# A transformer pair on one core: another order of the first products, the bias table's load, and the conditioning work beside attention

## The reference

```python
# first_block
mod = (c_act @ ada_w[i] + ada_b[i])[:, None, :]          # conditioning: 6 vectors of 1024
sh1, sc1, g1, sh2, sc2, g2 = jnp.split(mod, 6, axis=-1)
h = rmsnorm(x, mix_norm_pre[i]) * (1.0 + sc1) + sh1
y = windowed_gqa_sink(h, w_qkv, w_o, sink, rel_bias)     # 16 heads, bias table from rel_bias
x = x + g1 * rmsnorm(y, mix_norm_post[i])
h = rmsnorm(x, ffn_norm_pre[i]) * (1.0 + sc2) + sh2
y = (jax.nn.silu(a) * b) @ w_out                         # a, b = split(h @ w_in)
x = x + g2 * rmsnorm(y, ffn_norm_post[i])
# second_block: 2 layers; each ends in peer(): 16384 experts, 8 heads x top 16 for each token,
# whose rows are gathered from memory
```

## Time and profile before

| | us |
|---|---|
| median of 3 runs | 2074.97 (2071.8 to 2075.92) |
| the profiled execution, its own time | 2070.76 |
| span from its first to its last instruction | 2069.0 |
| PE / DVE / ACT / POOL busy | 1744.1 / 1469.1 / 919.5 / 613.1 |
| first Q, K, V matmul; first unit of attention on DVE; `post` | 37.5; 70.7; 156.9 |
| FFN's first product; its second; end of the second's matmuls | 171.5; 301.6; 363.3 |

### The profile page before, as it was taken

How to read it: one execution, slowest core, us unless ns; L and a number is a source line. 1 busy time by engine, 2 the same in 40 slices (tenths; PEclk the granted TensorE clock), 3 DMA queues, 4 the chain that set the end, 5 groups by cost and what they waited for, 6 DMA issues and landing times.

```text
span 2069.0 us, 21998 instructions
## 1 busy us (share of the span) xinstructions
PE 1744.1 (84%) x6989; PEld 1026.8 (50%) x6989; DVE 1469.1 (71%) x3271; ACT 919.5 (44%) x2397; POOL 613.1 (30%) x575
## 2 busy tenths in 40 slices
PE   3888999899888798987887787998999978778876
PEld 2657998788767354533322323464555423223322
DVE  6778877888876587766677767527776767667675
ACT  3555444444472344453444444334444444444443
POOL 1250000000002354433434343114455433433431
PEclk9998999999999999999999999999999999999999
DMA  9654768566645999999999999859999999999996
GB/s 380 267 193 182 265 245 305 215 256 243 242 166 205 418 421 422 421 421 417 421 421 422 421 421 421 325 188 384 408 418 421 421 422 421 422 421 421 422 421 256
DMA packets 114651, 723.24 MB, mean 350 GB/s; under 512 B 11484, under 2 KB 13300, under 8 KB 34024
## 3 DMA queue, kind: packets, MB, share of 16 engines
q0 software_dynamic: 75152, 541.35, 63.1%
q1 hardware_dynamic: 39384, 180.50, 23.5%
HBM read 720.72 MB, written 1.08 MB: 349 GB/s over the span
## 4 chain that ended last, share of the span: by engine, by line
DMA 38%; PE 30%; DVE 18%; ACT 7%; issue 4%; POOL 3%; SPq 0%; ACTq 0%; DVEq 0%
DMA X<-in_k_uv,EI 24%; DMA Z<-in_k_uv,EI 12%; PE PS L2266 12%; PE PS L1956 4%; PE PS L1958 4%; PE PS L1957 4%; DVE junk L1943 3%; DVE W L1568 3%; PE PS L2242 3%; DVE WL L1580 2%; POOL X L1074 2%; ACT WH L1083 1%; PE PS L2283 1%; ACT L1083 1%; ACT E L1083 1%
## 5 line engine op out<-in xcount | busy, mean ns | idle before, releaser
L2266 PE MATMUL PS<-X,dg 128*128 128x512 f32 x1380 | 666.7, 616 | 129.2 <-ACT dg L1083 128.5
L1943 DVE CUSTOM_DVE_ANT_0 junk<-H,X 128x1024 f32<-128x1024 f32 x345 | 421.9, 1223 | 240.6 <-DMA X<-in_k_uv,EI 235.9
L1074 POOL DMA_INDIRECT X<-in_k_uv,EI x345 | 364.8, 1057 | 512.5 <-PE PS L2266 378.1
L2266 PEld LDWEIGHTS PS<-X,dg 128*128 128x128 f32 x1380 | 249.2, 193 | 504.7 <-ACT dg L1083 289.1
L1083 ACT ACTIVATE CF<-DOT 128x1 f32<-128x1 f32 x512 | 103.6, 202 | 661.2 <-DVE DOT L1943 660.3
L2266 PE MATMUL PS<-Z,dg 128*128 128x512 f32 x480 | 237.6, 622 | 56.4 <-ACT dg L1083 55.9
L1943 DVE CUSTOM_DVE_ANT_0 junk<-H,Z 128x1024 f32<-128x1024 f32 x120 | 146.8, 1223 | 95.6 <-DMA Z<-in_k_uv,EI 93.8
L1083 ACT ACTIVATE dg<-CP,CG 128x128 f32<-128x128 f32 x512 | 205.5, 401 | 18.2 <-PE PS L2266 1.5
L1956 PE MATMUL PS<-XH,WH 128*128 128x256 f32 x592 | 174.5, 295 | 16.2 <-DVE XL L1483 14.8
L2266 PEld LDWEIGHTS PS<-Z,dg 128*128 128x128 f32 x480 | 84.5, 192 | 189.9 <-ACT dg L1083 123.2
L1957 PE MATMUL PS<-XL,WH 128*128 128x256 f32 x592 | 170.5, 288 | 0.0
(11 more groups left out here) (319 smaller groups left out, 2509.6 us busy)
## 6 DMA issues: line engine op xcount, KB each, us to landing
W<-in_k_ada SPq DMA_DIRECT2D x58, 1024.0 KB, 5.4
W<-in_k_win SPq DMA_DIRECT2D x15, 1024.0 KB, 5.7
Y<-in_k_ada SPq DMA_DIRECT2D x14, 1024.0 KB, 6.3
W<-in_k_ffi SPq DMA_DIRECT2D x14, 1024.0 KB, 5.5
Y<-in_k_ffi SPq DMA_DIRECT2D x8, 1024.0 KB, 6.6
W<-in_peer_wq SPq DMA_DIRECT2D x8, 1024.0 KB, 14.0
W<-in_ffn_w_out SPq DMA_DIRECT2D x6, 1024.0 KB, 7.6
W<-in_ab_w_out SPq DMA_DIRECT2D x6, 1024.0 KB, 6.2
```

The lines of the kernel that those rows point to most:

```text
L1074: e.indirect_dma_start(out=WS[k][:, :], out_offset=None, in_=I[f"k_uv{ly}"][:, :], in_offset=bass.IndirectOffsetOnAxis(ap=EI[t][:, j:j + 1 ...
L1943: e.tensor_tensor_reduce(junk, H[:, t, :], d[:, 0:D], 1.0, 0.0, ALU.mult, ALU.add, DOT[:, j:j + 1]).then_inc(v_dot, 1)
L2266: p = e.matmul(PS[:, 2 * t + q, :], dgb[n % 4][:, :], d[:, D + q * 512:D + (q + 1) * 512], start=(j == 0), stop=(j == 127))
```

## The change

1. **Start of the program.** `be` stands behind `ldw 1`, and POOL now waits there until `ldw 1` has landed. `ada 6 1`, `ada 7`, `mod 1` and `g 1` stand ahead of both halves of `split 0`, so on DVE they come before the first low part of weights. `split 0 0` stands behind `xt` of chunk 3, `split 0 1` behind chunk 5.
2. **Block 0** runs its quarters in the order 0, 2, 1, 3: both halves of the result over chunks 0 to 3, then both over 4 to 7. The second half is summed in another PSUM bank (2), from which the copy on ACT reads it.
3. **Attention.** The halves of blocks 6 and 7 move from steps 3 to 6 to steps 7, 8, 10 and 11, those of block 8 from 13, 14 to 14, 15. The `ada` operations move so that most steps hold either one half or one `ada`; the last steps hold two or three. `mod 3` and `g 2` stand just before the last output block.
4. **`ada 21`** moves from right before `post` into the FFN's first product, at blocks 3 and 7 of it, and **`ada 22`** from the FFN's second product to blocks 11 and 15.
5. **The FFN's second product.** Block i waits for activation pair i, no longer for all 11.

```diff
-    P("be")
     P("xp", 0, 7, 3)
...
     P("ldw", 1)
+    P("be")
     for c in range(3):
         P("xt", 0, c, first[c])
-    P("split", 0, 0)
+    ada(6, 1)
     for c in range(3):
         P("xl", 0, c)
-    ada(6, 1)
+    P("ada", 7, 0)
+    P("ada", 7, 1)
+    P("mod", 1)
+    P("g", 1)
     P("xt", 0, 3, first[3])
+    P("split", 0, 0)
     P("xl", 0, 3)
...
+        for q in (0, 2, 1, 3) if n == 0 else range(4):
+            P("gq", n, q, n)
...
-    halves = {1: (5, 0), 2: (5, 1), 3: (6, 0), 4: (6, 1), 5: (7, 0), 6: (7, 1), 13: (8, 0), 14: (8, 1), 17: (9, 0),
+    halves = {1: (5, 0), 2: (5, 1), 7: (6, 0), 8: (6, 1), 10: (7, 0), 11: (7, 1), 14: (8, 0), 15: (8, 1), 17: (9, 0),
...
-    adas = {0: [22, 23], 1: [24], 2: [25]} | {n: [n + 20] for n in range(6, 22)}
...
+            18: [34], 19: [35, 36, 37], 20: [38, 39], 21: [40, 41]}
...
-    ada(21, 0)
-    ada(21, 1)
     P("post", 0, 0)
...
-    late = [22, 23] + list(range(32, 39))
+    late = [23] + list(range(32, 39))
...
                     w.wait_ge(d_td, 16)
+                    w.wait_ge(*slot("ldw", 1)[1:])
                     e.dma_start(BE[:, :, :], bass.AP(tab_d, 0, [[1, 128], [512, 16], [1, 384]])).then_inc(d_be, 16)
...
-                        w.wait_ge(a_ff, 11)
-                        w.wait_ge(v_ffl, 11)
+                        w.wait_ge(a_ff, n - FO + 1)
+                        w.wait_ge(v_ffl, n - FO + 1)
```

More of the change, by code:

```diff
@@ L111, in make_plan @@
     P("ldw", 1)
+    P("be")
     for c in range(3):
         P("xt", 0, c, first[c])
-    P("split", 0, 0)
+    ada(6, 1)
     for c in range(3):
         P("xl", 0, c)
-    ada(6, 1)
+    P("ada", 7, 0)
+    P("ada", 7, 1)
+    P("mod", 1)
+    P("g", 1)
     P("xt", 0, 3, first[3])
+    P("split", 0, 0)
     P("xl", 0, 3)
-    P("split", 0, 1)
-    P("ada", 7, 0)
     for c in (4, 5):
@@ L124, in make_plan @@
         P("xl", 0, c)
-    P("ada", 7, 1)
-    P("mod", 1)
-    P("g", 1)
+    P("split", 0, 1)
     for c in (6, 7):
@@ L134, in make_plan @@
         ada(8 + n, 0)
-        gemm(n, n)
+        for q in (0, 2, 1, 3) if n == 0 else range(4):
+            P("gq", n, q, n)
         P("evac", n)
@@ L144, in make_plan @@
     fill |= {9 + 4 * i + q: [(WO + i, q)] for i in range(3) for q in range(4)}
-    halves = {1: (5, 0), 2: (5, 1), 3: (6, 0), 4: (6, 1), 5: (7, 0), 6: (7, 1), 13: (8, 0), 14: (8, 1), 17: (9, 0),
+    halves = {1: (5, 0), 2: (5, 1), 7: (6, 0), 8: (6, 1), 10: (7, 0), 11: (7, 1), 14: (8, 0), 15: (8, 1), 17: (9, 0),
               18: (9, 1), 20: (10, 0), 21: (10, 1)}
-    adas = {0: [22, 23], 1: [24], 2: [25]} | {n: [n + 20] for n in range(6, 22)}
+    adas = {0: [22, 23], 3: [24], 4: [25], 5: [26], 6: [27], 9: [28], 12: [29], 13: [30], 16: [31, 32], 17: [33],
+            18: [34], 19: [35, 36, 37], 20: [38, 39], 21: [40, 41]}
     for n in range(22):
@@ L169, in make_plan @@
             P("gc", 0)
-        elif n == 20:
-            P("mod", 3)
-            P("g", 2)
         if n < 16:
@@ L177, in make_plan @@
     P("ldw", FI + 1)
+    P("mod", 3)
+    P("g", 2)
     gemm(WO + 3)
-    ada(21, 0)
-    ada(21, 1)
     P("post", 0, 0)
@@ L187, in make_plan @@
     P("silu")
-    at = {i: d for d, i in enumerate((i for i in range(22) if i % 4 != 3), 48)}
+    at = {i: d for d, i in enumerate((i for i in range(21) if i % 4 != 3), 48)} | {
+        3: 42, 7: 43, 11: 44, 15: 45}
     for i in range(22):
@@ L191, in make_plan @@
         P("ldw", n + 2)
-        if i in at and at[i] < 64:
+        if i in at:
             ada(at[i] // 2, at[i] % 2)
@@ L203, in make_plan @@
         P("ldw", n + 2)
-        if i < 9:
+        if i < 8:
             ada(late[i], 0)
@@ L1182, in _ @@
                             o = QT[:, 2 * QKV_ORDER[n] + m, :].rearrange("p (t n) -> p t n", t=2)[:, :, ::-1]
-                            q = act(o, PS[:, b, m * 256:(m + 1) * 256].rearrange("p (t n) -> p t n", t=2), ACT.Copy,
+                            z = PS[:, b + (2 * m if n == 0 else 0), m * 256:(m + 1) * 256]
+                            q = act(o, z.rearrange("p (t n) -> p t n", t=2), ACT.Copy,
                                     scale=0.125)
@@ L1978, in to_t @@
                     z = slice(k * 256 + m * 128, k * 256 + m * 128 + 128)
-                    p = mm3(PS[:, b, m * 256:(m + 1) * 256], h[:, z], l[:, z], xh[:, k, :], xl[:, k, :], k == 0, k == 7)
+                    p = mm3(PS[:, b + (2 * m if n == 0 else 0), m * 256:(m + 1) * 256], h[:, z], l[:, z], xh[:, k, :],
+                            xl[:, k, :], k == 0, k == 7)
                 return p
@@ L2070, in _ @@
                             take(b)
+                            if n == 0:
+                                take(2)
+                                free[2] = [(a_ev, nth.ev[0])]
                         p = to_t(n, 0, b, q) if QKV_ORDER[n] < 5 else to_n(n, 0, b, q)
```

## The result

The changed kernel takes 2082.89 us (median of 6 runs, 2081.78 to 2086.7), the kernel before 2075.44 (6 runs, 2071.8 to 2076.54): ratio 1.0042, 95% interval 1.0029 to 1.0055, so 6 to 11 us slower. The prediction was 2071.5, range 2066.5 to 2076. Both the sign and the range missed.

What follows compares the result with a forecast made beforehand. Landing of gathered expert rows (36% of the span) is untouched; the front is bound stage by stage by differing engines and loads. Terms -2.8 + 1.1 + 0.45 - 2.27, taken as 3.5 off median 2074.97, give 2071.5 us; range 2066.5 to 2076.

Steps and rivals of the forecast that it cites:

- Block 0: Start of the program: PE begins about 37.6, runs unbroken and ends at 45.6 instead of 51.88, 6.2 us earlier.
- The loads: Before attention: `ada 11`'s load lands at 65.6, so DVE's first unit starts 2.8 us earlier; bounds 1.5 to 6.2.
- What an earlier start is worth later: From first unit to kernel end: whatever the front gains or loses was taken to arrive at the end unchanged.
- Attention: Steps 3 to 15 with the moved halves: together 1.1 us later (0.0 to 2.6), including 0.75 for PE's lower clock.
- The end of attention: Step 16 to `post`: 0.45 us later; bounds 1.5 earlier to 1.5 later.
- The FFN's second product: Starts at once without PE's wait for the last activations: 2.27 us earlier; bounds 1.5 to 2.3.
- The FFN's first product: Bound by PE, with over 1 us of DVE slack per 5.77 us, so four more products cost nothing.
- the late table: Slower rival, before attention: bias table lands near 85, first unit 14 us later than today, 2088 us; chance 0.08.
- the rival in which attention costs more: PE stays at the lower level in steps 9 to 11, or sums' order breaks: net gain 0 to 1.5; chance 0.20.

Runs made afterwards that it cites:

- e8_cb: Kernel before with the new start alone, and POOL's two broadcasts issued only after `ada 11`'s load has landed: 2073.67 us, ratio 0.9994.
- e10_all: Kernel before with the new start, broadcasts behind `ada 11`'s load, wait per activation pair, and `ada 21`, `ada 22` whole in blocks 7, 15: 2069.6 us, ratio 0.9969.
- e7_warm: `e3_att` with 12 more matmuls, whose sum nobody reads, at the end of each of attention steps 6, 7 and 8: 2082.05 us, ratio 1.0025.
- e3_att: Kernel before with the new attention tables and the new place of `mod 3` and `g 2` alone: 2080.4 us, ratio 1.0024.
- e6_715: Changed kernel with both halves of `ada 21` in block 7 and both of `ada 22` in block 15: 2074.24 us, ratio 0.9994.
- e5_hold: Kernel before with the halves of `ada 24` and `ada 25` reordered, so one slot is held four blocks, no work added: 2081.82 us, ratio 1.003.

## Why the prediction was wrong, point by point

**Block 0: right.** No gap, PE from 37.51 (I had 37.6), copy at 45.74 (45.6).

**The loads: right mechanism, half the size.** `ada 11` binds, and the table lands at 62.9 (61 to 63). Predicted 65.6 for the load, measured 66.4 to 67.2 in four traces. My sum had 24.32 + 1.05 = 25.37 MB moved at that time; in the changed kernel it was 26.12 MB at 67.2 us. Nearly all of POOL's was in by then (4.39 of 4.45 MB), as the sum had it; the 0.8 MB too many are the hardware queue's (21.68 MB, where I had 20.89), from loads issued behind `ada 11`'s, which I had left out. `e8_cb` and `e10_all` show that the broadcasts are worth 1 to 1.7 us, where I had 2.6 (65.6 against 63.0). First unit 69.10 on average of these four, 70.58 in the six without the new start: 1.5 earlier, not 2.8. That is my lower bound.

**What an earlier start is worth later: not in the sum at all.** I carried the gain of the first unit to the end unchanged. With the old tables, the stretch from first unit to `as` 15 took 63.1 us on average of four traces with the old start (62.2 to 64.5) and 64.7 of four with the new (64.5 to 65.1). The new start was 2.6 us ahead at the first unit, 2.2 at `as` 14 and 1.0 at `as` 15.

**Attention: the right term, priced at its low end.** Steps 3 to 6 were 2.85, 3.81, 2.68 and 2.85 us (I had 2.9, 3.7, 2.75, 2.75), the six with a half 5.15 to 5.36 (5.14), step 12 3.55 (3.55), step 13 3.21 (3.2). Step 9 took 5.64, for which I had 3.55, and "up to 2.6" if PE came into it cold, of which I took 0.75. `e7_warm` shows it was that; it took 3.56 there. New tables against old, with the old start: `as` 0 to 15 in 65.3 us (`e3_att`) against 63.1; I had 1.1.

**The end of attention: right.** From `as` 15 to `post` 25.3 us on average of three traces of the changed kernel's plan, 24.9 of five of the old: +0.4, predicted +0.45. The trace that I had read has 24.0, the low end of these five (24.0 to 25.6); that is also why 156.85 was early.

**The FFN's second product: right.** Its wait is gone, and nothing took its place.

**The FFN's first product: the step that failed.** It reads: "DVE has over 1 us of slack in each of its 5.77 us, so four more products cost nothing". DVE's time was the wrong account. The halves that moved there keep a slot from the load to the second half, for four blocks, and the loads behind them in the queue wait. The term was 0 and measured 11.3 (139.13 against 127.86). Whether the moved loads find their slots free, and whether the loads behind them do, I had asked for attention ("all slots free many microseconds ahead") and not here. All the range's bounds came from other terms, and the slower rival, the late table, was a mechanism that did not happen.

By averages of traces: -1.5 (first unit), +2.5 (`as` 0 to 15, 65.6 against 63.1), +0.4 (to `post`), +8.4 (FFN to its second product, 139.1 against 130.7 on average of five), together +9.8; the interval of the medians is 6 to 11. Without what the slots cost, the prediction would have come out within its range, on the side of its high end (`e6_715`: 2074.24), but not by its forecast: a gain of some 1 us, as in the rival in which attention costs more, since the start gave 1.5 instead of 2.8 and attention cost 2.5 instead of 1.1.

## What to carry to other kernels

Where loads take a ring of slots in turn, count for each load how many steps lie between the last use of its slot and its own first use, before and after a move. One operation in two halves far apart, or one load more that shifts the ring, can starve a stage in which every engine but the one that bounds it has slack.

A gain ahead of a stage is worth what the waits behind it leave. Follow it step by step: here 2.2 of 2.6 us were still there at `as` 14, and one step whose fill met TensorE at the lower clock took more than half of that.

Compare a stage over several traces of the same code before calling a microsecond a gain.

## What the runs showed of the hardware that I had not expected

Gaps of 2.23 and 2.44 us on PE within the FFN's first product (changed kernel) and one of 2.58 us (`e5_hold`) were each followed, at once or up to 1.4 us later, by some 3.4 us of matmuls at the pace of the lower level, 1.2 GHz (0.21 us apart instead of 0.12), which costs 1.5 us each. Gaps of 0.68 to 1.39 us were not, and neither was one of 3.06 us: behind it (214.38 in `e5_hold`) the granted clock stayed at 1.00. So the length of a gap alone did not decide it. With PE kept busy in the three idle steps of `e7_warm` the granted clock in 95 to 105 us was 1.00, where it had been 0.63.

Executions of the same instructions reached `post` up to 3.3 us apart (156.85 to 160.17), and most of that lies in stretches at the lower clock: from `as` 15 to `post` it was 24.0 us where the granted clock in 140 to 150 us was 1.00, and 25.5 where it was 0.83 to 0.90.
